# A gated mixer whose head outputs are made channel by channel: norms from sums spread by TensorE, the output product head by head, its weights loaded over the keys, and projection blocks in two banks

## The reference

```python
h = rms_norm(x, norm_g[i, 0]) * (1.0 + sc1) + sh1
proj = h @ w_in                                   # 1024 -> 5 * 1024
q, f_fw, f_bw, i_in, g = jnp.split(proj, 5, axis=-1)
...
o_fw = hgrn2_chunk_scan(q, k_fw, v, logf_fw)      # 8 heads of 128, chunks of 128 tokens
o_bw = rev(hgrn2_chunk_scan(rev(q), rev(k_bw), rev(v), rev(logf_bw)))
o = rms_norm(o_fw + o_bw, norm_g.reshape(HG_HEADS, HG_DV)) * jax.nn.silu(g)
x = x + g1 * (o.reshape(B, S, D_MODEL) @ w_out)
```

## Time and profile before

| | |
|---|---|
| median of 3 runs | 2485.41 us |
| the profiled execution, its own time | 2485.46 us |
| its span in the profile | 2483.8 us |
| TensorE busy | 2298.6 us (93%) |
| VectorE busy | 1756.2 us (71%) |
| ScalarE busy | 1227.2 us (49%) |
| mean granted TensorE clock | 0.967 of full |
| projection, from its first split product to its last copy | 413.86 to 547.19 us |
| attention stage | 547.5 to 612.5 us |
| mixer's output, first matmul to the last of the output product | 612.6 to 668.05 us |

### The profile page before, as it was taken

One profiled execution on the slowest core, in us unless ns is written; L12 is line 12 of the kernel. 1 busy time (PEld: TensorE's weight loads), 2 busy tenths in 40 slices (PEclk: granted clock), 3 DMA queues, 4 the chain that ended last, 5 costly groups with the idle time before them and its releaser, 6 DMA issues. The chain is left out here.

```text
span 2483.8 us, 46252 instructions
## 1 busy us (share of the span) xinstructions
PE 2298.6 (93%) x15780; PEld 1995.0 (80%) x15780; DVE 1756.2 (71%) x3159; ACT 1227.2 (49%) x1961; POOL 287.5 (12%) x289
## 2 busy tenths in 40 slices
PE   7979989977799999998999998699999999899997
PEld 7647746944499999997888887579999999788886
DVE  5764864757558887886666778566888888576766
ACT  4543543545244456554555444634445555454444
POOL 0000000000000000001332440100000000344432
PEclk9989999988899999998999998899999999999999
DMA  7554554665337776666777786234777664778775
GB/s 210 187 204 130 189 197 137 218 255 212 123 136 228 228 221 210 188 186 185 241 240 241 242 247 221 102 119 142 229 226 219 199 187 152 247 241 241 241 242 164
DMA packets 246822, 498.42 MB, mean 201 GB/s; under 512 B 57001, under 2 KB 133033, under 8 KB 243393
## 3 DMA queue, kind: packets, MB, share of 16 engines
q1 hardware_dynamic: 246720, 497.07, 62.6%
HBM read 462.34 MB, written 34.65 MB: 200 GB/s over the span
## 5 line engine op out<-in xcount | busy, mean ns | idle before, releaser
L2582 PE MATMUL psum<-split_operands 128*128 128x512 f32 x3072 | 701.8, 391 | 20.7 <-ACT split_operands L2561 20.7
L2582 PEld LDWEIGHTS psum<-split_operands 128*128 128x128 f32 x3072 | 579.7, 189 | 142.4 <-ACT split_operands L2561 21.0
L2320 PE MATMUL psum<-split_operands 128*128 128x256 f32 x4096 | 543.1, 286 | 8.8 <-ACT split_operands L2354 8.8
L2320 PEld LDWEIGHTS psum<-split_operands 128*128 128x128 f32 x4096 | 510.1, 192 | 10.2 <-ACT split_operands L2354 10.2
L2573 DVE TENSOR_TENSOR split_operands<-weights_ring,split_operands 128x1024 fp32r<-128x1024 f32 x256 | 314.8, 1230 | 223.3 <-ACT split_operands L2561 223.3
L2546 POOL TENSOR_TENSOR arena<-arena,residual_gates 128x256 f32 (+1 forms) x256 | 263.5, 1029 | 1684.8 <-DMA residual_gates<-expert_activations 1684.8
L2561 ACT CAST split_operands<-weights_ring 128x1024 fp32r<-128x1024 f32 x256 | 269.5, 1053 | 348.8 <-PE psum L2582 347.4
L2397 DVE TENSOR_TENSOR split_operands<-weights_ring,split_operands 128x1024 fp32r<-128x1024 f32 x256 | 313.2, 1223 | 101.2 <-ACT split_operands L2354 100.2
L318 PE MATMUL psum<-split_operands 128*128 128x256 f32 x2304 | 283.1, 285 | 8.0 <-DVE split_operands L333 5.7
L318 PEld LDWEIGHTS psum<-split_operands 128*128 128x128 f32 x2304 | 279.0, 192 | 10.9 <-DVE split_operands L333 5.0
L2324 PE MATMUL psum<-split_operands 128*128 128x256 f32 x2048 | 287.6, 283 | 0.0
(11 more groups left out here) (325 smaller groups left out, 2052.9 us busy)
## 6 DMA issues: line engine op xcount, KB each, us to landing
weights_ring<-in_peer_u_dram SPq DMA_DIRECT2D x256, 512.0 KB, 3.6
weights_ring<-in_peer_v_dram SPq DMA_DIRECT2D x256, 512.0 KB, 4.6
expert_activations<-residual_gates SPq DMA_DIRECT2D x256, 128.0 KB, 1.9
residual_gates<-expert_activations SPq DMA_DIRECT2D x256, 128.0 KB, 4.3
split_words<-in_w_ada_dram SPq DMA_DIRECT2D x20, 768.0 KB, 6.4
weights_ring<-in_w_in_dram SPq DMA_DIRECT2D x6, 2048.0 KB, 8.7
weights_ring<-in_hg_w_in_dram SPq DMA_DIRECT2D x5, 2048.0 KB, 7.9
arena<-in_hg_w_in_dram SPq DMA_DIRECT2D x5, 2048.0 KB, 7.8
```

The source lines that it names most:

```text
L2320: nc.tensor.matmul(K.ps[:, 4 + b, 0:SEQ], u_t[:, b, 0, k], h[:, wh, k], start=(k == 0 and wh == 0), stop=False)
L2582: return K.nc.tensor.matmul(K.ps[:, 4 + 2 * t + half], g[:, s, w, t * P:(t + 1) * P], vs[:, s % 2, wv, half * 512:(half + 1) * 512], start ...
```

## The change

Four things are changed, in all three stages.

In the projection, g is made with channels on the partitions (blocks 8 and 9 become "cols"), and leaves PSUM through Silu. "cols" blocks of this stage are packed: two 128x256 results share a bank, so that a block takes two banks and not four; of two that share one only the first starts with the flag that opens the bank. The modulation row goes into bank 2, its places are spread from block 4 on, its ring has three slots, and its loads are issued at n = 3, 6, 7 and 8.

In the attention stage, SP waits until VectorE has written its last exponents (`exps_q` at 8), loads `w_out` in two halves of 2 MB into the memory of the keys and of the running sums, and then stores only round 0 of the modulation row. Round 1 stays in bank 5 of PSUM, is copied out by ScalarE as its first work of the next stage, and is stored there by SP, ahead of the first load of the query weights.

In the queries stage `HgOut` is new. TensorE makes each head's output with channels on the partitions (2 matmuls of 128x256 per head). ScalarE squares four heads at once, TensorE multiplies the squares by a matrix of ones, which gives every partition the sum over the 128 channels, and ScalarE makes the factor from it as `Exp(-0.5 * Ln(sum / 128 + eps))`. VectorE makes output x gain x gate meanwhile, and its product with the factor is the h_t of the output product, head by head; TensorE makes the output product's four (t, n) of a head as the head comes, for heads 0 to 3 in all four banks, then heads 4 to 7 for t = 0, and last for t = 1, one column half after the other. There are no copies from PSUM, no transposes, and the norm gain is a column (4 KB).

The diff, without empty lines, the renamed flag at its other callers and the removed body of `HgOut`, which stands above at L1648 to L1727:

```diff
+    def __init__(self, K, sem, blocks, outs=None, early=4, wslot=None, packed=False):
+        self.K, self.blocks, self.outs, self.early, self.packed = K, blocks, outs, early, packed
...
+        self.copy_out(act, lambda out, src: self.K.nc.scalar.activation(out, src, self.outs[n]), n)
+    def columns(self, n, c):
+        b0 = self.banks(n)
+        if not self.packed:
+            return self.K.ps[:, b0 + c, 0:SEQ]
+        return self.K.ps[:, b0 + c // 2, (c % 2) * SEQ:(c % 2 + 1) * SEQ]
...
-                            last = nc.tensor.matmul(self.K.ps[:, b0 + c, 0:SEQ],
+                            last = nc.tensor.matmul(self.columns(n, c),
                                                     self.w[:, m % 4, a, c * P:(c + 1) * P],
-                                                    self.h[:, b, k], start=first, stop=last_one)
+                                                    self.h[:, b, k], start=first and not (self.packed and c % 2),
+                                                    stop=last_one, skip_group_check=self.packed)
                         else:
...
-        src = (self.K.ps[:, b0:b0 + 4, 0:SEQ] if kind == "cols" else
-               self.K.ps[:, b0:b0 + TT, 0:width])
+        if kind == "rows":
+            src = self.K.ps[:, b0:b0 + TT, 0:width]
+        elif not self.packed:
+            src = self.K.ps[:, b0:b0 + 4, 0:SEQ]
+        else:
+            src = self.K.ps[:, b0:b0 + 2].rearrange("p b (c t) -> p (b c) t", c=2)
...
-ROW_PLACES = [(6, 1), (6, 5), (7, 1), (7, 5), (8, 1), (8, 5), (9, 1), (9, 3)]
+ROW_PLACES = [(4, 5), (5, 3), (6, 1), (6, 6), (7, 3), (8, 1), (8, 5), (9, 2)]
+ROW_LOADS = {3: (0, 3), 6: (3, 5), 7: (5, 6), 8: (6, 8)}
...
-        product = SplitProducts(K, sem, blocks, scalar_outs=True, sigmoids=4)
+        outs = [ACT.Sigmoid] * 4 + [ACT.Copy] * 4 + [ACT.Silu] * 2
+        product = SplitProducts(K, sem, blocks, outs, packed=True)
-        row = ModulationProducts(K, sem, gates.area, gates.area, 1, 0, 1, 4, [6], c=(H.c, False),
-                                 ring=[K.arena[:, 24576:26624], K.arena[:, 26624:28672]])
+        row = ModulationProducts(K, sem, gates.area, gates.area, 1, 0, 1, 4, [2], c=(H.c, False),
+                                 ring=[K.arena[:, 24576:26624], K.arena[:, 26624:28672], gates.area.take(2048)])
...
-                elif n == 4:
-                    row.load(sp, 0, 2)
-                elif n == 8:
-                    row.load(sp, 2, 4)
-            row.load(sp, 4, 8)
+                elif n in ROW_LOADS:
+                    row.load(sp, *ROW_LOADS[n])
...
-    H.g = area.take(TT, D)
+    H.g = area.take(HG, CH, P)
...
+    H.w_out = [a.rearrange("p (k n) -> p k n", k=KD // 2) for a in (
+        H.k.rearrange("p d h c t -> p (d h c t)"), H.pre.rearrange("p d n t -> p (d n t)")[:, 0:4 * D])]
...
             mod.load(sp, 2, 16)
-            mod.store(sp)
+            sp.wait_ge(exps_q, NU)
+            w_out = K.i["hg_w_out_2"][0].rearrange("(k p) n -> p k n", p=P)
+            for half in range(2):
+                sp.dma_start(H.w_out[half], w_out[:, 4 * half:4 * half + 4]).then_inc(K.hg_out_loaded[half], 16)
+            mod.store(sp, 1)
...
-            mod.act_out(act, 1)
...
+        self.sq, self.z, self.factor = (area.take(HG, SEQ) for _ in range(3))
+        self.gain = area.take(HG)
+        self.row = area.take(512)
+        self.limit = 28672
+    def head(self, h):
+        return self.K.ps[:, h // 2, (h % 2) * SEQ:(h % 2 + 1) * SEQ]
+    def heads(self, half):
+        return self.K.ps[:, 2 * half:2 * half + 2].rearrange("p b (h t) -> p (b h) t", h=2)
+    def sums(self, half):
+        b0 = (6, 0)[half]
+        return self.K.ps[:, b0:b0 + 2]
     def sp(self, sp):
+        load_cols(sp.dma_start, self.gain, self.K.i["hg_norm_g_2"], HG).then_inc(self.g_loaded, 16)
+        sp.wait_ge(self.row_ready, 1)
+        for q in range(4):
+            dst = self.K.mod_dram[1:2, bass.ds((8 + q) * 512, 512)]
+            sp.dma_start(dst, self.row[32 * q:32 * q + 1]).then_inc(self.stored, 16)
     def sp_done(self, sp):
+        sp.wait_ge(self.stored, 64)
+        for half in range(2):
+            sp.wait_ge(self.K.hg_out_loaded[half], 16)
         sp.wait_ge(self.o_ready, 2 * TT)
     def pe(self, pe):
         K, H, nc = self.K, self.H, self.K.nc
+        def heads(hs):
+            for h in hs:
                 for s in range(TT):
+                    last = nc.tensor.matmul(self.head(h), H.v[:, s, h * P:(h + 1) * P],
+                                            H.at[:, h, 2 * s:2 * s + 2].rearrange("p c t -> p (c t)"),
                                             start=(s == 0), stop=(s == 1))
             last.then_inc(self.heads_ready, 1)
+        def sums(half):
+            pe.wait_ge(self.sq_ready, half + 1)
+            for b in range(2):
+                h = 4 * half + 2 * b
+                last = nc.tensor.matmul(self.sums(half)[:, b], K.ones[:],
+                                        self.sq[:, h:h + 2].rearrange("p h t -> p (h t)"), start=True, stop=True)
+            last.then_inc(self.sums_ready, 1)
+        def output(t, n, k):
+            return nc.tensor.matmul(K.ps[:, 4 + 2 * t + n], K.h_t[:, k, t * P:(t + 1) * P],
+                                    H.w_out[k // 4][:, k % 4, n * 512:(n + 1) * 512],
+                                    start=(k == 0), stop=(k == KD - 1))
+        heads(range(0, 4))
+        heads(range(4, 6))
+        sums(0)
+        heads(range(6, 8))
+        pe.wait_ge(K.hg_out_loaded[0], 16)
+        pe.wait_ge(self.row_ready, 1)
+        for k in range(4):
+            pe.wait_ge(self.y_ready, k + 1)
+            for t in range(TT):
+                for n in range(2):
+                    output(t, n, k)
+            if k == 0:
+                pe.wait_ge(self.z_ready, 1)
+                sums(1)
+        pe.wait_ge(K.hg_out_loaded[1], 16)
+        for k in range(4, KD):
+            pe.wait_ge(self.y_ready, k + 1)
+            for n in range(2):
+                last = output(0, n, k)
+                if k == KD - 1:
+                    last.then_inc(self.o_ready, 1)
+        for n in range(2):
+            for k in range(4, KD):
+                last = output(1, n, k)
+            last.then_inc(self.o_ready, 1)
     def act(self, act):
+        K, nc = self.K, self.K.nc
+        def squares(half):
+            act.wait_ge(self.heads_ready, 1 + 2 * half)
+            nc.scalar.activation(self.sq[:, 4 * half:4 * half + 4], self.heads(half), ACT.Square
+                                 ).then_inc(self.sq_ready, 1)
+        def factors(half):
+            mine = self.factor[:, 4 * half:4 * half + 4].rearrange("p h t -> p (h t)").rearrange(
+                "p (b n) -> p b n", b=2)
+            act.wait_ge(self.sums_ready, half + 1)
+            nc.scalar.activation(mine, self.sums(half), ACT.Ln, scale=1.0 / HD, bias=K.eps[:]
+                                 ).then_inc(self.ln_ready, 1)
+            act.wait_ge(self.ln_ready, half + 1)
+            nc.scalar.activation(mine, mine, ACT.Exp, scale=-0.5).then_inc(self.factor_ready, 1)
+        for q in range(4):
+            ins = nc.scalar.copy(self.row[32 * q:32 * q + 1], K.ps[32 * q:32 * q + 1, 5])
+        ins.then_inc(self.row_ready, 1)
+        squares(0)
+        factors(0)
+        squares(1)
+        factors(1)
     def dve(self, dve, link):
+        K, H, nc = self.K, self.H, self.K.nc
         dve.wait_ge(self.g_loaded, 16)
+        for half in range(2):
+            dve.wait_ge(self.sq_ready, half + 1)
+            for h in range(4 * half, 4 * half + 4):
+                ins = nc.vector.scalar_tensor_tensor(
+                    self.z[:, h], self.head(h), self.gain[:, h:h + 1], H.g[:, h].rearrange("p c t -> p (c t)"),
+                    ALU.mult, ALU.mult)
+            ins.then_inc(self.z_ready, 1)
+            dve.wait_ge(self.z_ready, half + 1)
+            dve.wait_ge(self.factor_ready, half + 1)
+            for h in range(4 * half, 4 * half + 4):
+                nc.vector.tensor_tensor(K.h_t[:, h], self.z[:, h], self.factor[:, h], ALU.mult
+                                        ).then_inc(self.y_ready, 1)
...
-    for part, dst in ((3, H.v), (4, H.g)):
-        for half in range(2):
-            blocks.append(("rows", part * D + half * 512, 512, dst[:, :, half * 512:(half + 1) * 512]))
+    for half in range(2):
+        blocks.append(("rows", 3 * D + half * 512, 512, H.v[:, :, half * 512:(half + 1) * 512]))
+    for half, hs in enumerate(half_heads):
+        blocks.append(("cols", 4 * D + half * 512, 512, H.g[:, hs].rearrange("p h c t -> p h (c t)")))
...
-        assert tail.area.at <= 24576
+        assert tail.area.at <= tail.limit
```

More of the change, by code:

```diff
@@ L361, in dve @@
                 self.dve_weights(dve, n * KD + k)
-                if k == 3 and not self.scalar_outs:
+                if k == 3 and self.outs is None:
                     self.copy_out(dve, self.K.nc.vector.tensor_copy, n - 1)
@@ L365, in dve @@
```

(10 more changed lines are left out.)

77 lines of the change are left out of this document (10 added, 67 removed).

## The result

The changed kernel takes 2470.35 us (median of 4 runs, 2468.48 to 2473.16) against 2485.54 before (median of 4, 2483.99 to 2488.71): a ratio of 0.9932, 95% interval 0.9921 to 0.9944, 15.2 us less. Measured once more, beside the experiments, it was 2470.27 and 0.9934 (0.9920 to 0.9948). Forecast were 2465.7 within 2458 to 2472.5.

A forecast was written before the change was run, and what follows sets the result against it. TensorE was taken as near full in the projection apart from two weight waits, with one engine at a time working in the output. From 2485.46 us, -8.6 - 2.3 - 13.3 + 1.9 + 2.5 = -19.8 gave 2465.7, range 2458 to 2472.5.

The forecast's parts named there:

- Part 1: Projection: both TensorE waits for the modulation row's weights go, less small additions; -8.6 us, between -8.8 and -4.
- rival D: Projection: row loads starve block 4's load; at 300 GB/s it comes 4 us late, total 2471.4 us; chance 0.10.
- the gate by columns: Projection: making blocks 8 and 9 as column blocks adds 0.1 us each, 0.2 us.
- Part 2: End of attention stage: without round 1's copies and stores the next stage begins sooner; gain 2.3 us, between 0.7 and 4.5.
- VectorE bounds the rest of that stage, which the change leaves alone: Attention stage: apart from the copies and stores at its end, VectorE sets the time; no change counted there.
- rival A: End of attention stage: round 0's stores not held by the weights, turnover at 608.1, total 2463.5 us; chance 0.12.
- Part 3: Output stage: norm and output product overlap the heads, 42.2 us instead of 55.4; -13.3 us, between -16.4 and -11.6.
- rival E: Output stage: no overlap, the output product waits for all eight heads; total 2473.1 us; chance 0.05.
- the cold start: Output stage: heads start at half clock after a gap of 3 us; a warm start would save 1.8 us.
- (608.0 - 612.6): Output stage: trace times given for half of the heads' columns being done at 5.4 us.
- Part 4: Handover to the next layer: t = 1's diagonal comes later, +1.9 us, and half clock behind the idle time, +2.5 us.
- Rival B: Heads' start and handover: TensorE stays warm through 3 and 3.6 us of idle; up to 4.3 less, 2461.4 us; chance 0.14.

The follow-up runs named there:

- e3: Changed kernel with the modulation row's products and loads back at their old places and two slots instead of three: 2477.27 us.
- e1: Changed kernel with the 4 MB of output weights loaded at the start of the output stage instead of in the attention stage: 2465.77 us.
- e11: The same kernel as e1, measured again side by side with the changed kernel: 2464.94 us.
- e5: e1 plus a square root of a constant column behind ScalarE's last Exp, so the handover's table loads early: 2463.83 us.
- e6: e1 with VectorE's handover order changed: t = 1's residual halves moved ahead of weight chunks, the fourth chunk behind t = 1's diagonal: 2465.36 us.
- e7: e1 with both the early table load of e5 and the new VectorE order of e6: 2462.38 us.
- e8: Changed kernel with the Exp of the norm's factor replaced by a second Ln, so no table changes between the two: 2468.87 us.
- e10: The changed kernel itself, measured again side by side with e9 and e11: 2470.27 us.
- e2: The kernel before, with the same 4 MB of weights also loaded at the attention stage's last exponents and used by nobody: 2490.94 us.
- e9: Changed kernel with the first 2 MB of output weights loaded in the attention stage, the second 2 MB at the output stage's start: 2465.73 us.

## Why the prediction was right and where it was not

**Part 1** (-8.6, measured -7.87). The row loads were in time: no wait of TensorE for them, none for block 4, so rival D is out. The waits were worth 8.80 (e3) where the sum had 8.76. The mis-sized term is the gate by columns: "8 x (1.448 - 5.74 / 4) = 0.1 us each, 0.2" measured 0.93. The trace after shows where the rest is. Between two of the row's products, stretches of 4, 5 and 6 column chunks (from 516.05, 522.96 and 471.08) take 5.94, 7.38 and 8.82 up to the next start: 1.44 a chunk, as in the long row, and 0.18 once. Stretches of 4 and 5 row chunks take 5.67 and 7.03: 1.36 a chunk and 0.23 once. So a column chunk costs 0.08 more than a row chunk, which 5.74 / 4 hid by spreading what is paid once; 16 x 0.08, less 0.05 for each of some four stretches, is an estimate of 1.1.

**Part 2** (-2.3, measured +2.89) is where the prediction failed. The failed step is "VectorE bounds the rest of that stage, which the change leaves alone". The 4 MB were priced for what stands behind them on SP's queue, the stores, and that mechanism came true and did no harm: the weights were through about 602, 13 us behind their issue as in the sum, SP waited 10.9 us for round 0's stores, to about 602.8 (so rival A is out), and T came at 608. The sum didn't ask what else uses the DMA engines. TensorE's code does, and its late fetches made TensorE the last engine of the stage. e1 without the load has -3.30 in this stage, within the stated bounds of -4.5 to -0.7. So the forecast of the stage holds but for one effect, which cost 6.2 us in the trace (67.94 against 61.75) and 5.3 in the medians.

**Part 3** (-13.3, measured -14.56). The order of events is as worked out. TensorE idles once, 2.47 us ahead of the output (2.2 forecast), and then not until the end; rival E is out. The mis-sized term is the cold start: the heads were to start at half clock and cost 1.8 more, for "a gap of 3 us is left". The gap was 0.44 us, as TensorE had worked until 607.70 and the stores no longer ended the stage. The clock was back at full early in the heads (24 matmuls in 5.70; 5.42 where it was full from T, in e1, whose gap was 0.74). The working's "(608.0 - 612.6)" is a slip for 618.08 of the earlier trace rows; its 5.4 is right.

**Part 4** (+4.4, measured +3.84). The diagonal came 5.18 behind TensorE's end, 5.4 forecast, the transposes ran at 3.78 as in the earlier trace rows, the 144 products took 18.53.

**Rival B**, the warm clock, was not put to the test in part 3, where the idle time of 3 us that it speaks of didn't come about, and did not come true in part 4. That is not a matter of the idle time alone, as the last section shows: e11 has the warm clock there.

The total lay inside the range and 4.65 above the forecast. Part 2's miss of 5.2 was not balanced by the others (+0.7, -1.3, -0.6); the sum of the four is 4.1 above the forecast's. The other 0.55 is less than single runs of a kernel differ by. That the total still fell into the range is owed to the range's width: part 2 by itself lay outside its own bounds, with the wrong sign.

## What to carry to other kernels

A bulk load that is moved into a stage where its target is free isn't free itself: it shares the DMA engines with the engines' own code. In this kernel a stretch with many short instructions on an engine (128 products of 32 columns in 1.5 us) is where a late fetch shows, as idle time on "issue" with no releaser. Put such a load where the engine runs few and long instructions, as in the output stage, where the same 4 MB did no harm (40.59 in e1). Around a handover look first at what comes in front of the last-needed operand (table loads, work for later), since idle time there may cost as much again in clock.

## What the runs showed of the hardware

**Bulk loads hold up TensorE's instructions.** 4 MB in flight turned an idle time of 1.9 to 2.2 us (e1, e5, e6, e7, e11) into 4.1 to 4.6 (after, e3, e8, e10), and one of 0.35 into 3.41 (e2 against before). A packet of instructions that was due started up to 2.6 us later, and TensorE went on 1.2 to 1.6 us behind its end. The stall in the changed kernel ended 2 us after the weights had gone through.

**The clock after an idle time is not a function of its length.** The same 3.2 us in the handover was followed by half clock in e1 and by full clock in e11, the same kernel. It isn't the chip: e10, on e11's chip, has 3.78 behind the same 3.24. The timeline of TensorE in the two, e1 first:

```profile
649.92 3.78 PE L203 MATMUL psum<-arena,x_rows 128*128 128x128 f32 x16 [3.23 <-DVE arena L183]
```

```profile
654.42 2.05 PE L203 MATMUL psum<-arena,x_rows 128*128 128x128 f32 x16 [3.24 <-DVE arena L183]
```

The same 2.47 ahead of the output was followed by full clock in after and in seven other profiles (3.67 for eight records of matmuls) and by half in e9 (5.37). Single profiles of one kernel can thus differ by 2 us in each such place: from the transposes to the next scores e1 took 26.92 and e11 24.81. The Trainium skill (TensorE: Matmul & The Clock Gate, What's actually happening) says of the start of a kernel that the number of cold matmuls varies from run to run. These pairs, in the middle of one, vary too, by 2.1 and 1.7 us. A forecast should hold both outcomes of such a gap in its range, and a comparison of single traces should take it out first.
